# Second layer's two own modulations behind the seventh and eighth up tile, each sum in two parts on VectorE

## What is computed

```python
sc = silu(c)
mod = sc @ w_mod[layer] + b_mod[layer]            # 6 * 1024 values
shift1, scale1, gate1, shift2, scale2, gate2 = split(mod, 6)
h = rmsnorm(x, g_attn) * (1 + scale1) + shift1
x = x + gate1 * mixer(h)                          # attention, w_in and w_out
h = rmsnorm(x, g_mlp) * (1 + scale2) + shift2
u, g = split(h @ w_up, 2)                         # 2816 columns each
g = causal_depthwise_conv(g, conv_w, conv_b)      # three taps along the tokens
x = x + gate2 * ((silu(g) * u) @ w_down)
```

## Time and profile before

| what | us |
| --- | --- |
| median of 3 runs | 2014.02 |
| lowest and highest | 2012.65, 2014.62 |
| the profiled execution | 2012.51 |
| its span in the trace | 2010.7 |
| TensorE, VectorE, GpSimd busy in it | 1612.7, 695.3, 153.9 |
| second layer's up tiles, start of j = 2 to start of j = 9 | 606.09 to 710.75 |

### The profile page before, as it was taken

One profiled execution on the slowest core, in us unless ns is written; L12 is line 12 of the kernel. 1 busy time (PEld: TensorE's weight loads), 2 busy tenths in 40 slices (PEclk: granted clock), 3 DMA queues, 4 the chain that ended last, 5 costly groups with the idle time before them and its releaser, 6 DMA issues.

```text
span 2010.7 us, 20617 instructions
## 1 busy us (share of the span) xinstructions
PE 1612.7 (80%) x8516; PEld 868.9 (43%) x8516; DVE 695.3 (35%) x1438; ACT 298.4 (15%) x805; POOL 153.9 (8%) x105
## 2 busy tenths in 40 slices
PE   7999999999997999998765565656998765565665
PEld 3466988544677974574221121211574221121211
DVE  1574556977538676264010010101164010010101
ACT  1143000011610100353000010000253000010000
POOL 0000000000014740220000000000220000000000
PEclk9999999999998999999878788887999887787878
DMA  9790888755236442745899999999745999999997
GB/s 341 288 364 8 276 290 293 281 200 178 85 102 221 166 164 85 215 168 232 361 421 421 422 422 422 422 422 412 217 167 230 369 421 422 421 422 422 422 422 311
DMA packets 184333, 599.64 MB, mean 298 GB/s; under 512 B 18752, under 2 KB 77760, under 8 KB 135104
## 3 DMA queue, kind: packets, MB, share of 16 engines
q1 hardware_dynamic: 184014, 598.03, 76.5%
q10 hardware_dynamic: 242, 0.53, 0.1%
HBM read 594.75 MB, written 3.80 MB: 298 GB/s over the span
## 4 chain that ended last, share of the span: by engine, by line
PE 56%; DMA 37%; DVE 5%; ACT 1%; issue 1%; DVEq 0%; POOL 0%; SPq 0%; ACTq 0%; POOLq 0%
DMA extra<-in_w_down 13%; DMA extra<-in_w_up 13%; DMA extra<-in_w_gate 10%; PE ps L1176 9%; PE ps L1525 7%; PE ps L1287 6%; PE ps L1240 6%; PE ps L1212 4%; PE ps L884 4%; PE ps L1032 4%; PE ps L1425 3%; PE ps L1121 3%; DVE extra L2221 2%; PE ps L998 1%; PE ps L775 1%
## 5 line engine op out<-in xcount | busy, mean ns | idle before, releaser
L1525 PE MATMUL ps<-ring,wide 128*32 128x512 f32 x2240 | 345.5, 773 | 223.6 <-DMA ring<-in_w_down 91.6
L1525 PEld LDWEIGHTS ps<-ring,wide 128*32 128x32 f32 x2240 | 82.8, 137 | 467.8 <-issue 219.3
L1525 PE MATMUL ps<-extra,wide 128*32 128x512 f32 x784 | 138.7, 843 | 92.7 <-DMA extra<-in_w_down 34.8
L2977 DVE TENSOR_TENSOR wide<-ps,wide 128x512 f32<-128x512 f32 x16 | 10.3, 686 | 512.4 <-PE ps L1525 512.4
L1176 PE MATMUL ps<-hT,ring 128*128 128x256 f32 (+1 forms) x1088 | 183.8, 331 | 0.0
L1176 PEld LDWEIGHTS ps<-hT,ring 128*128 128x128 f32 x1088 | 166.8, 191 | 17.1 <-issue 2.9
L1287 PE MATMUL ps<-ring,hT 128*128 128x512 f32 (+2 forms) x320 | 127.3, 555 | 0.3 <-issue 0.3
L1525 PEld LDWEIGHTS ps<-extra,wide 128*32 128x32 f32 x784 | 31.9, 148 | 198.3 <-issue 84.8
L2221 DVE SCALAR_TENSOR_TENSOR extra<-ring,sc,extra 128x512 f32<-128x512 f32 x140 | 115.1, 822 | 5.0
L2982 DVE COPY wide<-ps 128x512 f32<-128x512 f32 x8 | 5.5, 692 | 294.4 <-PE ps L1525 294.4
L884 PE MATMUL ps<-ring,hT 128*128 128x512 f32 x192 | 88.2, 619 | 2.0 <-ACT hT L1605 2.0
(11 more groups left out here) (362 smaller groups left out, 2024.7 us busy)
## 6 DMA issues: line engine op xcount, KB each, us to landing
ring<-in_w_gate SPq DMA_DIRECT2D x24, 4096.0 KB, 34.0
ring<-in_w_down SPq DMA_DIRECT2D x24, 4096.0 KB, 34.1
ring<-in_w_up SPq DMA_DIRECT2D x22, 4096.0 KB, 33.1
ring<-in_w_mod SPq DMA_DIRECT2D x24, 2048.0 KB, 13.8
ring<-in_w_up SPq DMA_DIRECT2D x44, 1024.0 KB, 7.8
extra<-in_w_gate SPq DMA_DIRECT2D x8, 4096.0 KB, 33.5
extra<-in_w_up SPq DMA_DIRECT2D x8, 4096.0 KB, 34.4
extra<-in_w_down SPq DMA_DIRECT2D x8, 4096.0 KB, 33.6
```

The source lines that it names most:

```text
L1525: last = mm(ps[bank + n][e * CAP:(e + 1) * CAP, :], lhs[:, k, e * CAP:(e + 1) * CAP], expert_at(n0, e, k % PAIR, n * N), start=k == 0, sto ...
```

## The change

`LAG` becomes a pair, `LAGS = (2, 6)`: layer one is as before, and the second layer's two mod tiles stand behind up tiles j = 6 and j = 7, in the order of loading, on TensorE, and in `mod_out` on VectorE. The sums are made elsewhere too: q = 0 behind the products of j = 3 (row blocks 0 to 3: the TENSOR_SCALAR and three SCALAR_TENSOR_TENSOR) and j = 4 (blocks 4 to 7: four SCALAR_TENSOR_TENSOR), q = 1 behind those of j = 5 and j = 6. No operation is added or taken away.

```diff
-LAG = 2
+LAGS = (2, 6)
...
-            if LAG <= n < len(late) + LAG:
-                tiles.append((late[n - LAG][0], "mod", late[n - LAG][1]))
+            if LAGS[l] <= n < len(late) + LAGS[l]:
+                tiles.append((late[n - LAGS[l]][0], "mod", late[n - LAGS[l]][1]))
...
-                    if j - LAG < late:
-                        modulation(EARLY[L] + j - LAG)
+                    if 0 <= j - LAGS[L] < late:
+                        modulation(EARLY[L] + j - LAGS[L])
...
-                def accumulate(q):
+                def accumulate(q, ks=range(KD)):
...
-                    ts(acc[:, q % 2, :], wt[:, 0, :], csil[:, 0:1], None, ALU.mult).then_inc(s.up(), 1)
-                    for k in range(1, KD):
+                    if ks[0] == 0:
+                        ts(acc[:, q % 2, :], wt[:, 0, :], csil[:, 0:1], None, ALU.mult).then_inc(s.up(), 1)
+                    for k in ks[ks[0] == 0:]:
...
-                    if LAG <= j < late + LAG:
-                        mod_out(EARLY[L] + j - LAG)
+                    if LAGS[L] <= j < late + LAGS[L]:
+                        mod_out(EARLY[L] + j - LAGS[L])
                     if j == UPT - 1:
                         down_sums(1)
-                    if L <= j < late + L:
-                        accumulate(EARLY[L] + j - L)
+                    if L == 0 and j < late:
+                        accumulate(EARLY[L] + j)
+                    if L == 1 and 3 <= j < 3 + 2 * late:
+                        accumulate((j - 3) // 2, range(4) if j % 2 else range(4, KD))
                 if L == 0:
```

More of the change, by code:

```diff
@@ L1243, in down @@
                     return last
-                pe.wait_ge(*s.at("b1_mod_ready", EARLY[L] + min(late, UPT - 1 - LAG)))
+                pe.wait_ge(*s.at("b1_mod_ready", EARLY[L] + min(late, UPT - 1 - LAGS[L])))
                 for j in range(DOWN_TAIL[0]):
@@ L1252, in _ @@
                             if L == 0:
-                                pe.wait_ge(*s.at("b1_mod_ready", EARLY[L] + UPT - LAG))
+                                pe.wait_ge(*s.at("b1_mod_ready", EARLY[L] + UPT - LAGS[L]))
                         if j == 0 and m == 3:
@@ L1257, in _ @@
                     last.then_inc(tile_done, 1)
-                    if UPT + j - LAG < late:
-                        modulation(EARLY[L] + UPT + j - LAG)
+                    if UPT + j - LAGS[L] < late:
+                        modulation(EARLY[L] + UPT + j - LAGS[L])
                 for j in DOWN_TAIL:
@@ L2631, in _ @@
                     product(j)
-                    if LAG <= j < late + LAG:
-                        mod_out(EARLY[L] + j - LAG)
+                    if LAGS[L] <= j < late + LAGS[L]:
+                        mod_out(EARLY[L] + j - LAGS[L])
                     if j == UPT - 1:
                         down_sums(1)
-                    if L <= j < late + L:
-                        accumulate(EARLY[L] + j - L)
+                    if L == 0 and j < late:
+                        accumulate(EARLY[L] + j)
+                    if L == 1 and 3 <= j < 3 + 2 * late:
+                        accumulate((j - 3) // 2, range(4) if j % 2 else range(4, KD))
                 if L == 0:
-                    mod_out(EARLY[L] + UPT - LAG)
+                    mod_out(EARLY[L] + UPT - LAGS[L])
                 down_sums(2)
@@ L2643, in _ @@
                     accumulate(EARLY[L] + UPT)
-                    mod_out(EARLY[L] + UPT + 1 - LAG)
+                    mod_out(EARLY[L] + UPT + 1 - LAGS[L])
                 down_sums(5)
@@ L2647, in _ @@
                 if L == 0:
-                    mod_out(EARLY[L] + UPT + 2 - LAG)
+                    mod_out(EARLY[L] + UPT + 2 - LAGS[L])
                     ab(1, 0, "g_attn")
```

## The result

The median is 2021.17 us (2018.85 to 2023.34, 7 runs) against 2014.62 (2012.65 to 2016.61, 7 runs): 6.6 us slower, ratio 1.0033, 95% interval 1.0021 to 1.0044. The forecast was 6.9 us slower. The profiled execution has a span of 2017.3 us, 6.6 more than before.

A forecast was written before the change was run, and what follows sets the result against it. TensorE was taken to hold 56% of the chain, weight loads 37%, VectorE 5%. Removed waits and new waits behind GpSimd-held VectorE work moved up tile j = 9 from 710.75 to 717.6: 6.9 us slower, 2021.0 us, range 2009 to 2024.

The forecast's parts named there:

- The cost of an operation beside GpSimd: VectorE's sums: one operation gets through for each of GpSimd's sums of weights, 2.74 us each against 0.78 with GpSimd idle.
- T(2): Start of up tile j = 2 on TensorE, 606.09 us in the profile before; the stretch judged begins here.
- The taps beside GpSimd: VectorE's six taps of j = 4 start 1 us behind GpSimd; each of GpSimd's four operations lets one through.
- the second rival: VectorE's taps are not held by GpSimd: 4.4 us faster, chance 0.10; only two held: no change, chance 0.10.
- The first rival: Two VectorE operations pass for each of GpSimd's: 3.6 us slower in all, 2017.6 us; chance 0.22.
- The fourth, the low clock: Low TensorE clock behind gaps at j = 6, 7 delays GpSimd: 9.3 us slower; 0.50 together with the forecast.
- J + 15.4: Forecast end of a tile's product on VectorE, J being the start of that tile's join (646.8 for j = 4).
- The wait ahead of the last modulation: TensorE waits about 8 us for the sum q = 1, ready at 702.6, after tile j = 7 ends at 694.7.
- The prize: Gain if VectorE hid its sums altogether: 11.1 us of waits plus modulation and low-clock terms, 14.3 us.
- The sum: Whole effect at the start of up tile j = 9 on TensorE: 717.6 against 710.75 before, 6.9 us slower.
- the 13.71: Length in us of the up tile behind TensorE's first wait for a sum, at clock 0.92, against 12.51 normally.
- The third rival: VectorE has room: a 3.1 us half sum fits its idle time, all waits go, 14.3 us faster; chance 0.08.

The follow-up runs named there:

- after_few: Changed kernel with GpSimd's sums of weights in the second layer's up tiles cut from 128x1024 to 128x16 elements; 1996.99 us, ratio 0.9910 to the kernel before.
- two_ops: Changed kernel with only two operations in each of the four parts of its sums, the others left out; 2010.07 us, ratio 0.9977 to the kernel before.
- one_op: Changed kernel with only one operation in each of the four parts of its sums, the others left out; 1995.62 us, ratio 0.9904 to the kernel before.
- gp_late: Changed kernel where GpSimd starts its last sum of a tile only after the previous tile's taps; 2018.85 us, ratio 1.0019 to the kernel before.

## Why the prediction was right, and where it was not

- **The cost of an operation beside GpSimd** (2.74 us, 0.78 alone) was right, and the forecast rests on it. The first half sum was put at 8.8 us and took 8.9; the join of j = 4 was put at 646.8 and started at 646.27 with everything 0.54 earlier from T(2) on; the first gap was put at 1.7 us and was 1.46.
- **The taps beside GpSimd**, for which no row of before stood, are held, as the sum's operations are. Ten us in place of 2.7 settles the second rival (taps not held, or only the two TENSOR_SCALAR). The rule of the Trainium skill, page SBUF — State Buffer, section "SBUF: two separate sides", on two inputs in SBUF is borne out for the three-operand taps (10.14 us for four at j = 5, in place of 1.79). The TENSOR_SCALAR taps have only one input in SBUF beside a column, and they were held as well (1.59 and 2.44 us; in after_few both together take 0.74). The prediction quotes that rule for a mode that uses both ports too; no row shows which mode they ran in.
- **The first rival** (two operations get through for each of GpSimd's) falls: the taps come in independent pairs and still pass one by one.
- **The fourth, the low clock**, came true, and a term of the forecast that was too long hid it. Behind the gap of 5.18 us block 2 took 3.57 us in place of 1.79, at granted clock 0.50, the lower of the two levels (1.2 and 2.4 GHz); behind 1.46 us it stayed at 1.00. So GpSimd started 4.3 us behind the join in the next two tiles, not 2.5. For j = 4, at the high clock, the product ended at J + 14.8 where J + 15.4 was put: GpSimd's four operations followed each other every 2.4 us (648.87 to 658.50), not every 2.65. For j = 5 and j = 6 it ended at J + 15.8, while in two_ops, whose clock stayed up behind its gaps there, it ended at J + 14.8 in both. The low clock thus cost 1.0 us in each of two tiles, near the 1.2 of the rival, and the forecast was 0.6 us too long in each of three. Periods: 17.95 and 18.5 us, and 19.65 to the end of the last sum; put were 18.5, 18.2 and 19.1. That the sum of the three, 56.1, came so near the 55.8 of a forecast without the low clock is luck. The gaps ahead of block 2 of j = 6 and j = 7, put at 6 and 4 us, were 5.18 and 3.01.
- **The wait ahead of the last modulation** was put at 8 us and was 5.45, because tile j = 7 itself was longer at the low clock: its block 2 took 3.57 us and the block behind it at 686.76 took 2.91, and it ended at about 697.0, not 694.7; TensorE's end doesn't depend on it, as VectorE's sum sets it.
- **The sum**: T(9) was put at 717.6 and came at 717.70; counted from T(2), 6.9 us more were expected and 7.5 came. That the two times of T(9) agree to 0.1 us is luck as well, since T(2) was 0.54 us earlier. The loads cost nothing: TensorE had no wait for one in the stretch.
- **The prize** was put at 14.3 us and is 15.1. The term that was too small is the modulation: without a gap ahead of it the next tile starts 0.86 us behind it (668.59 to 669.45 in one_op), not 1.19, since its two records overlap the tile. That is 2 x 0.33; the rest is the overlap of records at the ends of tiles: I left 0.16 us of it out of each gap, and counted it once in the 13.71, which from start to start is 13.55.
- **A reading** was wrong. The join from 624.24 to 627.63 was given as proof that reads of PSUM are free of GpSimd, but GpSimd was idle then, from 619.84 to 631.11. The point itself holds by other rows: in the changed kernel the three reads from 624.96 took 1.47 us with a GpSimd operation beside them from 624.44 to 627.24.
- **The wording of the cause** was too narrow. I wrote of taps that escape GpSimd by a hair; gp_late shows that with the taps safe the half sum pays instead. Adding up both engines' times, as the expectation of gp_late does (some 16 us in a tile of 12.5), is not the measure either: without a sum that gives 9.8 + 2.7 + 0.7 = 13.2 us, in tiles of 12.51 without a gap, and the changed kernel's period is 18. What the rows show is a chain. For j = 4 it is 2.6 us from the start of the join through block 2 to GpSimd's start, 9.6 for its four operations, 2.6 to the end of the product and 3.1 for the half sum, 17.95 in all. The third rival compared 3.1 us with VectorE's idle 4.5 us and left GpSimd out of it.

## What to carry to other kernels

Before work is moved into an engine's idle time, ask what that idle time lies beside: VectorE's was there, but under GpSimd, and an operation cost three times its own length or more. Where two engines exclude each other, follow the chain through both for one period and compare it with the period's length. Splitting the sums in halves didn't help, since the first half still landed beside GpSimd and pushed the taps behind GpSimd's start. A pipeline that is exactly in step can fall out of it for several periods through one operation of 0.8 us more in each part (one_op against two_ops), so look for the place where both engines have nothing to do, here 13 us ahead of the first up tile.

## What the hardware showed that was not expected

- Back-to-back operations of VectorE that don't depend on each other pass GpSimd one at a time too: the two TENSOR_SCALAR taps of j = 4 took 1.59 and 2.44 us, 0.74 together in after_few, and the four others of j = 5, two independent pairs, 10.14 in place of 1.79.
- The cost is one-sided: GpSimd's operation beside a waiting one of VectorE took 2.35 to 2.83 us against 2.35 alone, while VectorE's, when it waited for a whole one of GpSimd's, took 2.3 to 2.8 against 0.4 to 0.8.
- Reads of PSUM in the join kept their 0.42 us beside GpSimd (1.47 for three at 624.96 in the changed kernel and at 667.37 before).
- TensorE's clock stayed up behind gaps of 1.46, 1.98 and 2.30 us (the block behind took 1.89 in the changed kernel and in two_ops) and was down behind one of 2.58 us in gp_late (3.40 for the block, clock 0.53), one of 3.01 us here (3.57, from 683.19 to 686.76, clock 0.50) and the longer ones.
